# Sums of squares with 64 columns of ones, exponentials issued a block later, and eight parts of units moved behind the triangular inverses, in a fused two-block kernel on one core

## The reference, cut to what matters

```python
def first_block(x, mem, ...):
    mem_n = rms_norm(mem, mem_norm_g)
    h = rms_norm(x, norm_g)
    proj = einsum("bsd,de->bse", h, dn_w_in)            # q, k, v, gates, xq, z
    mix = deltanet_branch(proj[..., :DN_MIX_COLS], ...)
    xa = memory_cross_attention(xq, mem_n, w_kv, ...)   # head norms of q and k, 4 heads
    y = concatenate([mix, xa]) * silu(z)
    return x + einsum("bse,ed->bsd", y, w_out)

def deltanet_branch(p, ...):
    qkv = silu(causal_depthwise_conv(p[..., :c_qkv], conv_w))
    q, k = l2_norm(q), l2_norm(k)                       # 12 heads of 128, 24 for v
    o = gated_delta_rule(q, k, v, g, beta)
    return rms_norm(o, out_g)

def gated_delta_rule(q, k, v, g, beta):                 # chunks of 64 tokens
    decay = exp(where(incl, gc[..., :, None] - gc[..., None, :], -inf))
    kk = einsum("bhncd,bhnjd->bhncj", k, k)
    m = where(strict, beta * kk * decay, 0) + eye(C)
    sol = triangular_solve(m, concatenate([v * beta, k * beta * exp(gc)]))
    ...
```

## Time and profile before

| | |
|---|---|
| median of three runs | 2964.25 us (2955.44 to 2966.82) |
| the profiled execution | 2971.03 us, span 2969.2 us |
| TensorE busy | 2828.3 us, mean granted clock 0.977 |
| VectorE, ScalarE, GpSimd busy | 1924.1, 1372.6, 389.8 us |
| instructions | 46176 |

### The profile page before, as it was taken

The page is one execution under the profiler, slowest core; times in us unless marked ns, Lnnn a source line. Parts: engine busy times, 40 slices in busy tenths (PEclk is TensorE's granted clock), DMA queues, the critical chain, the costliest instruction groups (busy, mean ns, idle before and its releaser), DMA issues.

```text
span 2969.2 us, 46176 instructions
## 1 busy us (share of the span) xinstructions
PE 2828.3 (95%) x19298; PEld 2664.3 (90%) x19298; DVE 1924.1 (65%) x2862; ACT 1372.6 (46%) x2243; POOL 389.8 (13%) x360
## 2 busy tenths in 40 slices
PE   6999989899999999999989999998999999999996
PEld 6999989889999998999979999997888899987775
DVE  5546648644445444655458666767878888878786
ACT  5346544445555334444344114443555555555454
POOL 0000010211111000005000002222122111112310
PEclk9999989999999999999989999999999999999998
DMA  4444444423324554544435469998999988899883
GB/s 188 171 156 142 171 133 163 163 89 114 113 96 157 185 181 150 183 152 158 157 110 178 167 209 361 360 345 336 367 360 369 342 326 319 325 351 351 328 335 143
DMA packets 109679, 668.46 MB, mean 225 GB/s; under 512 B 25776, under 2 KB 26312, under 8 KB 31552
## 3 DMA queue, kind: packets, MB, share of 16 engines
q1 hardware_dynamic: 83808, 496.08, 46.0%
q0 software_dynamic: 24512, 164.97, 15.1%
q10 hardware_dynamic: 1152, 4.47, 0.4%
HBM read 651.54 MB, written 13.30 MB: 224 GB/s over the span
## 4 chain that ended last, share of the span: by engine, by line
PE 65%; DMA 14%; DVE 13%; ACT 5%; issue 3%; POOL 0%; SPq 0%; DVEq 0%; ACTq 0%
PE PS L1036 64%; DMA raw<-in_pv 7%; DVE WL L1651 5%; DMA m<-in_pun,keep 4%; DVE m L1642 3%; ACT WH L2359 3%; DMA m<-in_pv,keep 2%; DVE m L2184 1%; ACT m L2344 1%; PE PS L1039 1%; DVE m L1851 1%; DMA raw<-in_w_kv 1%; DVE m L1848 0%; ACT m L2345 0%; DVE m_896r L2277 0%
## 5 line engine op out<-in xcount | busy, mean ns | idle before, releaser
L1651 DVE TENSOR_TENSOR WL<-raw,WH 128x1024 fp32r<-128x1024 f32 x804 | 985.7, 1234 | 605.9 <-ACT WH L2359 605.1
L2359 ACT CAST WH<-raw 128x1024 fp32r<-128x1024 f32 x804 | 837.2, 1046 | 570.7 <-PE PS L1036 393.2
L1036 PE MATMUL PS<-m_4096r,WH 128*128 128x256 f32 x5184 | 989.2, 292 | 29.4 <-DVE m L1642 14.7
L1036 PEld LDWEIGHTS PS<-m_4096r,WH 128*128 128x128 f32 x5184 | 821.2, 195 | 52.3 <-DVE m L1642 16.1
L1036 PE MATMUL PS<-m_4096r,WL 128*128 128x256 f32 x2592 | 739.8, 285 | 0.0
L1036 PE MATMUL PS<-m_8192r,WH 128*128 128x256 f32 (+1 forms) x2560 | 563.1, 314 | 15.5 <-issue 11.1
L1036 PE MATMUL PS<-WH,m_896r 128*128 128x512 f32 x1536 | 523.5, 393 | 27.5 <-DVE m_896r L2277 27.2
L1036 PEld LDWEIGHTS PS<-m_4096r,WL 128*128 128x128 f32 x2592 | 503.5, 194 | 0.0
L1036 PEld LDWEIGHTS PS<-m_8192r,WH 128*128 128x128 f32 x2560 | 400.2, 195 | 18.6 <-issue 11.7
L1036 PE MATMUL PS<-m_8192r,WL 128*128 128x192 f32 (+1 forms) x1792 | 406.0, 273 | 0.0
L1036 PE MATMUL PS<-WL,m_896r 128*128 128x512 f32 x1024 | 401.5, 392 | 0.0
(11 more groups left out here) (237 smaller groups left out, 1842.3 us busy)
## 6 DMA issues: line engine op xcount, KB each, us to landing
raw<-in_pu SPq DMA_DIRECT2D x128, 1024.0 KB
raw<-in_pv SPq DMA_DIRECT2D x128, 1024.0 KB
raw<-in_w_qkv SPq DMA_DIRECT2D x48, 1024.0 KB
raw<-in_w_o SPq DMA_DIRECT2D x48, 1024.0 KB
raw<-in_w SPq DMA_DIRECT2D x40, 1024.0 KB
raw<-in_w_z SPq DMA_DIRECT2D x32, 1024.0 KB
raw<-in_w_kv SPq DMA_DIRECT2D x16, 1024.0 KB
raw<-in_w_q SPq DMA_DIRECT2D x16, 1024.0 KB
```

What stands on the lines that cost most here:

```text
L1036: return e.matmul(o, l, x, start=start, stop=stop)
L1651: tt(WL[:, k, :], raw[:, n % NRAW, h * 1024:h * 1024 + 1024], WH[:, k, :].bitcast(F), ALU.subtract).then_inc(S["lo"], 1)
L2359: e.copy(WH[:, k, :], raw[:, n % NRAW, h * 1024:h * 1024 + 1024]).then_inc(S["hi"], 1)
```

## The change

(a) `add_up` replaces the products with one column of ones in `hn_sum`, `rn_sum` and `dn_yss`. It multiplies by 64 columns of ones and writes 64 equal columns from the target's column on; the next product begins one column further and writes over 63 of them. (b) `cross` gives one more `yield` between the norm of q and the first score. (c) `qk_norm` gives a `yield` after every second call of `rn_sum` instead of every sixth, two more ahead of `iv_turn` and one more behind it, and `mix` advances one part at each instead of three: 12 + 5 = 17 parts in place of 18. (d) ScalarE's relu and exponential get a name of their own, `iv_exp`. `iv_exp(0)` comes two parts after the second difference, `iv_exp(1)` two parts after the third, `iv_exp(2)` two parts later; the differences stand four parts apart instead of three. (e) From the first difference to the first scaling there are 3 x 4 + 9 = 21 parts instead of 3 x 3 + 20 = 29, and after `iv_out` 36 instead of 28.

```diff
--- before.py
+++ after.py
@@ -237,6 +237,7 @@
 
     def cross(self):
         yield from self.head_norm("q")
+        yield
         for h in range(4):
             for p in range(2):
                 self.do("ca_score", h, p)
@@ -249,10 +250,13 @@
     def qk_norm(self, st):
         for i in range(24):
             self.do("rn_sum", i)
-            if i % 6 == 5:
+            if i % 2 == 1:
                 yield
         self.do("rn_root")
+        yield
+        yield
         self.do("iv_turn")
+        yield
         yield
         yield
         st["n"] = True
@@ -279,8 +283,12 @@
         self.do("iv_store")
         for b in range(3):
             self.do("iv_decay", b)
-            yield 3
-        yield 20
+            yield 2
+            if b:
+                self.do("iv_exp", b - 1)
+            yield 2
+        self.do("iv_exp", 2)
+        yield 9
         for b in range(3):
             self.do("iv_scale", b)
             yield 4
@@ -288,7 +296,7 @@
             self.do("iv_step", j)
             yield 4 if 4 <= j < 27 else 2
         self.do("iv_out")
-        yield 28
+        yield 36
 
     def group(self, g, st):
         self.do("dn_in", g)
@@ -334,8 +342,7 @@
         st = {"v": 0, "n": False, "g": 0, "z": set(), "y": set(), "p": set()}
         fz = self.vz(st)
         for _ in self.qk_norm(st):
-            for _ in range(3):
-                next(fz)
+            next(fz)
         for parts in self.invert():
             for _ in range(parts):
                 next(fz)
@@ -1037,6 +1044,10 @@
 
             def tr(o, i):
                 return e.transpose(o, i, C("ident"))
+
+            def add_up(bank, c, x, start=True, stop=True):
+
+                return mm(PS[:, bank, c:c + 64], x, C("ones")[:, 0:64], start, stop)
 
             def spread(o, column, x):
                 return mm(o, column.to_broadcast([128, 128]), x, True, True)
@@ -1219,8 +1230,7 @@
                 for h in range(4):
                     for t in range(2):
                         for i in range(2):
-                            m = mm(PS[:, 2, 2 * h + t:2 * h + t + 1], tile(SQ, 2 * h + i)[:, tok(t)], C("ones")[:, 0:1],
-                                   i == 0, i == 1)
+                            m = add_up(2, 2 * h + t, tile(SQ, 2 * h + i)[:, tok(t)], i == 0, i == 1)
                 m.then_inc(S["hn_sum"], 1)
 
             def hn_spread(which):
@@ -1295,7 +1305,7 @@
                 p.wait_ge(*at("ca_exp", 7))
                 x = sq_tile(unit)
                 for t in range(2):
-                    m = mm(PS[:, 2, 2 * i + t:2 * i + t + 1], x[:, tok(t)], C("ones")[:, 0:1], True, True)
+                    m = add_up(2, 2 * i + t, x[:, tok(t)])
                 if i == 23:
                     m.then_inc(S["rn_sum"], 1)
 
@@ -1420,7 +1430,7 @@
                 bA = dn_bank(g)[0]
                 need_g(g, "ysq")
                 for i in range(4):
-                    m = mm(PS[:, bA, i:i + 1], blk(dn(g, "kb"), i), C("ones")[:, 0:1], True, True)
+                    m = add_up(bA, i, blk(dn(g, "kb"), i))
                 mark(g, "yss", m)
 
             def dn_ybc(g):
@@ -2486,7 +2496,7 @@
                 crossed(a)
                 e.copy(IV_GB, PS[0:48, 2, 0:256]).then_inc(S["iv_gates"], 1)
 
-            def iv_decay(b):
+            def iv_exp(b):
                 x = iv_e[:, b, :, :]
                 a.wait_ge(*at("iv_gap", b + 1))
                 a.step(act(x, x, ACT.Relu))
@@ -2722,7 +2732,7 @@
                   "mk_out": mk_out, "hn_sum": hn_sum, "mv_out": mv_out, "ab_out": ab_out, "sg_exp": sg_exp,
                   "sg_post": sg_post, "xq_out": xq_out, "ca_score": ca_score, "ca_value": ca_value, "qk_out": qk_out,
                   "v_out": v_out, "z_out": z_out, "rn_root": rn_root, "iv_turn": iv_turn,
-                  "iv_decay": iv_decay, "dn_decay": dn_decay, "dn_uc": dn_uc, "dn_w": dn_w, "dn_u": dn_u_, "dn_y": dn_y, "dn_yss": dn_yss,
+                  "iv_exp": iv_exp, "dn_decay": dn_decay, "dn_uc": dn_uc, "dn_w": dn_w, "dn_u": dn_u_, "dn_y": dn_y, "dn_yss": dn_yss,
                   "y_split": y_split, "x1_out": x1_out, "qi_out": qi_out, "index": index, "kq_out": kq_out,
                   "v2_out": v2_out, "aw": aw, "av": av, "pu_out": pu_out, "pm": pm, "dev": dev, "ln1": ln1, "h2": h2,
                   "h_out": h_out, "qs_out": qs_out, "s_exp": s_exp, "u_sum": u_sum, "u_out": u_out, "g_hots": g_hots, "g_apply": g_apply,
```

## The result

| | before | after |
|---|---|---|
| median | 2965.53 us (2955.44 to 2971.87, 4 runs) | 2943.61 us (2935.69 to 2944.77, 4 runs) |
| the profiled execution | 2971.03 us | 2935.69 us, span 2933.9 us |
| mean granted clock | 0.977 | 0.985 |

What follows compares the result with a forecast made beforehand. TensorE was busy 95% of the span, so time could come only from its idle and half-clock stretches. Gains 7.6 + 1.5 + 3.0 + 14.2 + 2.6 = 28.9 us from 2967.6 gave 2938.7 us, range 2927 to 2956.

Steps and rivals of the forecast that it cites:

- Clock in the sums: In the norm of q and k, 64 columns of ones remove the half-clock time of the sums of squares: 7.6 us.
- Rival A: The clock doesn't follow the width of the ones, so 9.1 us of gain are missing: 2947.8 us; chance 0.14.
- Clock behind the first head norm: After the first head norm, the wider ones remove a half-clock stretch of 3.4 us: 1.5 us gained.
- Query norm: Three unit steps ahead of the first score remove TensorE's whole 2.99 us wait; the softmax chain still ends ahead.
- Gates and differences: Root, transposition of gates and reading them back for the first difference stay hidden: no gain.
- Exponentials: Later exponentials replace TensorE's 9.05 us idle time with a 2.6 us wait, at 17.5 us after the first difference.
- Scaling 22.4 us after the difference: VectorE starts the scaling then instead of 35.4 us; the stored products land by 21.3 us, hidden by 1.1 us.
- rival B: The scaling waits for the stored products, landing 8 us later than counted: gain 20.9 us, 2946.7 us; chance 0.13.
- VectorE's stretch 94.7 us: From scaling to inverse VectorE sets the time, 94.7 us instead of 96.5; TensorE's idle and slow time there costs nothing.
- TensorE 20.1 us behind the inverse, last by 0.6: TensorE reaches the first group after the inverses' load, the 5.24 us wait goes, and the group starts 14.2 us earlier.
- Slow clock behind the wait for the inverses: With the wait for the inverses' load, the 5.7 us slow stretch after it goes: 2.6 us gained.
- rival C: Units and groups fall out of step; mild: half the gain lost, chance 0.07; in full: 2987.7 us, chance 0.04.

Runs made afterwards that it cites:

- e2: The kernel before with 64 columns of ones and nothing else changed: 2955.6 us, ratio 0.9967.
- e1: The kernel after with one column of ones again in place of 64, still in pairs: 2948.97 us, ratio 0.9940.
- e6: The kernel after without the new yield between the query norm and the first score: 2947.31 us, ratio 0.9952.
- e8: The kernel after with 40 parts instead of 36 behind the inverses: 2922.80 us, ratio 0.9874.
- e7: The kernel after with 37 parts instead of 36 behind the inverses: 2945.58 us, ratio 0.9937.
- f2: The kernel after with 44 parts instead of 36 behind the inverses: 2943.55 us, ratio 0.9936.
- e3: The kernel after with each exponential directly behind its difference again and the same parts: 2950.83 us, ratio 0.9930.
- f3: The kernel before with 31 parts instead of 28 behind its inverses and nothing else: 2949.99 us, ratio 0.9953.
- e9: The kernel after with two yields instead of one between the query norm and the first score: 2938.57 us, ratio 0.9938.

## Why the prediction was right, and where its steps failed

The time lay inside the range and 4.9 us above the forecast. That it came so near is partly luck: the terms for the query norm and for the inverses were too large by 6.3 us together, the gain of clock in the groups' stage was larger than counted, and a loss called unlikely came in part.

- *Clock in the sums*, predicted 7.6 us: 7.8 (0.7 of it is the part less). Rival A fell: the clock is 1.00 in the windows above, and e2, which has nothing but the width, shows it too. What the text left out is that the pairs would have done it without the width. *Clock behind the first head norm*, predicted 1.5: 1.3 us. The Trainium skill, page TensorE: Matmul & The Clock Gate, section What's actually happening, sets the clock by how busy the engine has been. e1 disagrees with it once more: the clock was halved at 109.5 us with TensorE busy for 4.40 of the 4.40 us ahead.
- *Query norm*, predicted 3.0: 1.2 us. The failed step is "which only shifts by three steps and still ends ahead": the softmax chain was late as well, behind the same VectorE, and 1.81 us of waiting moved there.
- *Gates and differences*, predicted nothing: nothing; no engine waits for the gates.
- *Exponentials*. The chain was right: the gate unit's silu ended 19.7 us after the difference (predicted 20.1) and TensorE waited 2.75 us (2.6) from 17.0 us on (17.5).
- *Scaling 22.4 us after the difference*: 25.1. The cover of 1.1 us wasn't enough; the products' load landed 16.3 us after its issue where the longest before was 12.7. This is rival B at 3.1 us of waiting instead of 8. In e1, e6 and e8 the wait is 0.83, 0.61 and 0.18 us and the scaling comes after 22.1 to 22.8 us, so the chain was counted rightly and the landing was not. Part of it is scatter: e7, e8 and f2 have the same instructions up to there and waited 2.67, 0.18 and 1.96 us. Part is not: with the later exponentials no trace has a longest landing under 13.5 us, while before, e2, e3 and f3 have 11.8 to 13.1. Why is open.
- *VectorE's stretch 94.7 us*: 94.7 to the store of the inverse (422.31 to 516.98), with seven convolutions in it, as counted, but 30 splits and 9.9 us of waits for casts instead of 32 and 11.2.
- *TensorE 20.1 us behind the inverse, last by 0.6*: 22.05 us (516.98 to 539.03), with no wait for the load. That "idle and slow time inside it costs nothing" held: in the kernel after, TensorE was idle for 6.5 us and at half clock for 6.8 us in that stretch, in e3 for 2.8 us and not at all, and in both 179 matmuls were left between the store of the inverse and the first group. It is the same 179 in e1, e6 and e9; with one, four and eight parts more it is 185, 203 and 227. The failed step is the count 14.3 + 5.8, which took TensorE's place at the inverse as fixed. Before, 117 matmuls were left with 28 parts behind, so eight parts more should make 165, and it was 179: with the stretch shifted by nine parts the inverse ends at another place in a unit, and TensorE, which gets its halves from VectorE's splits, stood 14 matmuls further back (1.7 us). The scaling 2.7 us too late and TensorE 1.95 us too late make the 9.7 us instead of 14.2.
- *Slow clock behind the wait for the inverses*, predicted 2.6, and nothing for the groups' ones: the stage had 19.2 us at half clock before and 6.8 us in e2 and in the kernel after, a gain of 5.6 us. How much of it a wait, the ones or the single execution made is open. In the kernel after none of it is seen, since the shift by one part brought rival C in its mild form: 6.2 us more idle (10.6 to 16.8), and 0.7 us for the part that is left. The failed sentence is "Later stages see the same work from an earlier start". The text named the mechanism (40 parts, five units, a shift by one) and gave its mild form 7 in 100; it took one bad meeting of 4.9 us for the norm and a shift of one part in eight for small. It didn't see that a shift could also gain 15 us, as the place four parts on does.

Sum of what was found: 1.3 + 1.2 + 7.8 + 9.7 - 1.5 = 18.5 us at matmul 7000, 20.2 at matmul 14400, and 21.9 in the medians. The last 1.7 are inside the scatter of the expert stage.

## What to carry over

When two streams are interleaved by fixed counts, try the offset between them by itself before anything else: here one number, four parts, was worth 15 us, two thirds of what the whole change gave, and three parts were worth 11 to 15 us in the kernel before. One-column products on TensorE lost the clock here where 24 to 32 stood in a row (in all but one place); 64 columns kept it there, and so did one column in rows of eight between wide products, and either edit alone was enough. A long wait is worth what it delays on the engine that sets the stage: 9 us of idle TensorE beside a chain of VectorE gave back 1.5 us at the first group, 4 at best.

## What the runs showed of the hardware beyond what was expected

- Products with 64 columns of ones cost next to no more time than with one: 32 take 3.68 us in the kernel after (103.89 us) and 3.63 us with one column in e1 at full clock (104.84 us), 0.115 and 0.113 us each.
- The two loads of the products, with the same bytes and behind the same instructions, landed at the latest 13.5 us after their issue in e8, 15.9 in e7 and 16.3 in the kernel after; before it was 12.7 us. A cover of 1 us over the longest landing of one profile was no cover.
- The expert stage has lengths 12 to 15 us apart in executions of nearly the same program. No experiment was made on it; its cause stays open.
